# Order of mixer work and weight splits on ScalarE and VectorE in a hybrid decoder layer, with the joined moves of slots, banks and gate rows

## The chip, the cores and the metric

One core of one Trainium2 chip. The metric is the device time of one launch in microseconds, median of the runs shown. Activations, weights and states are fp32.

## The reference, cut to what matters

One inference step of one layer: RMSNorm, one wide projection, two token mixers side by side (gated DeltaNet with 8 heads, mLSTM with 8 heads), a gated merge, an output projection, and a gated ConvFFN. There are 256 prompt tokens (fresh state) and 8 sample sequences of 4 tokens that continue a state.

```python
proj = h @ w_in
g_qkv, g_z, g_a, g_b, m_qkv, m_i, m_f, m_o, gate_a, gate_b = jnp.split(proj, idx, axis=-1)
c, new_gdn_conv = _causal_dwconv(g_qkv, gdn_conv_buf, gdn_conv_w)
c = jax.nn.silu(c)
...
go, new_gdn_S = _gated_delta_chunked(gq, gk, gv, g, beta, gdn_S.astype(f32))
go = _rmsnorm(go.transpose(0, 2, 1, 3), gdn_norm_w) * jax.nn.silu(g_z...)
y_a = go.reshape(B, T, GDN_V).astype(x.dtype) @ w_branch_a
...
mh, new_C, new_n, new_m = _mlstm_chunked(mq, mk, mv, ig, lf, ...)
y_b = mh.astype(x.dtype) @ w_branch_b
mixed = jax.nn.sigmoid(gate_a) * y_a + jax.nn.sigmoid(gate_b) * y_b
x = x + mixed @ w_out
```

## The kernel before, in words

All 288 tokens (256 prompt, 32 sample) lie along the free axis, so activations are stored transposed, 128 channels to a tile. A weight matmul multiplies a 128x128 block of weights by a 128x288 block of activations, and is done as three matmuls of rounded parts (`product`, lines 1914 to 1916): high weight part by high activation part, high by low, low by high.

**Weights.** SP loads them in units of 16 blocks of 128x128 into `w_raw`. Four of these blocks are one ring block. For each, ScalarE (ACT) makes the high part, `split_hi` (line 633, `w_hi`), VectorE (DVE) makes the low part, `split_lo` (line 640, `w_lo`), and PE multiplies. The ring has four places: in slot s, ACT and DVE make the block of slot s+3, once PE is through with slot s-1 (semaphore `blocks`). So three blocks lie ready ahead of PE at most.

**The front stage** is the projection by `w_in` with both mixers woven in: 384 slots of 12 matmuls each, four slots to a tile of 128 columns, 16 to a quad of four tiles. `ORDER` gives the quads: DeltaNet heads (q, k, v, z), mLSTM heads, and at the end gates. A finished tile is taken out of PSUM and scaled by DVE (`evacuate`, line 1484) in the first slot behind it; a consumer waits by `in_place(kind, i, m)` until tile m of a quad (0 to 3) is out.

Each engine has its own hand-written program for the front, and `front(eng, each, lanes, lanes_first)` (line 483) weaves it: in each slot it runs `each(slot)` (the engine's weight work) and lets every lane go on up to this slot. A lane is a generator, and `yield n` means that what follows is due n slots behind the lane's start. Lanes are `gates_rows` (from slot 0), `prepare(h)` for DeltaNet head h (from slot 17+28h), `scan(h)` (from 45+28h) and `mlstm(i)` (from 274+14i). Below, "phase n" is n slots behind a lane's start. On PE the lanes of a slot come ahead of its products, on ACT and DVE the weight split comes ahead of the lanes, and POOL has only lanes. A scan of head h runs in the same 28 slots as the preparation of head h+1: phase n of one is phase n of the other.

Names that the change and the steps touch:

- `prepare`: POOL copies the last columns of q, k, v (lines 774, 775), from which PE takes the convolution's state rows (line 1895); DVE and ACT form the convolution (lines 1521, 988), ACT applies Silu to it and to z (lines 1003 to 1008, with a table load ahead and one behind, 1000 and 1009); the squares' low part `sq_lo` (line 1524) feeds the norms on PE (line 1977); then come six levels of a triangular inverse, in which DVE forms `x_xt`, `decay` and `nt` (lines 1595, 1587) and PE multiplies pairs (lines 2012, 2018, 2021).
- `scan`: PE forms the output's sums (`nrm`, line 2075, from `sqo_lo`, line 1632); ACT makes the reciprocal root in two steps `rs1` and `rs2`; DVE scales by it (`go`, three instructions, line 1637); POOL multiplies by z (`goz`, line 820); ACT and DVE make the high and low parts of the result (line 1648 the low one). PE forms the state's update for 8 sequences (`Ss`, line 2085), and DVE adds it in, eight instructions `S_sample` (line 1644); ACT starts the stores of the states.
- `gates_rows`: DVE's row work on the mLSTM gates (lines 1414 to 1447), ACT's exponentials, and PE's turning of rows to columns (`cols`, `cols2`).

**Behind the front** comes the branch stage (`w_branch_a`, `w_branch_b`): each of its products' accumulators is a PSUM bank, `ps[:, 2 * (u % 2) + k % 2]`, which DVE's `first` and `second` multiply by the gates (lines 1736, 1742). The out stage (`w_out`) follows, and then the ConvFFN, which the change does not touch.

Of the kernel before, what the change touches and what calls it, by code (L numbers as in the profile page):

```python
# [7 lines left out]
P = 128  # L8
# [57 lines left out]
def build(nc, a, o):  # L66
# [3 lines left out]
    KT = D // P  # L70
# [56 lines left out]
    with ctx:  # L127
# [238 lines left out]
        scan_d = Steps(sem("scan_dve"), "S0 R1 S1 rs sql go ss1 ss2 lo")  # L366
# [116 lines left out]
        def front(eng, each, lanes, lanes_first=False):  # L483
            for slot in range(SLOTS):
                if lanes_first:
                    for lane in lanes:
                        lane.upto(slot)
                each(slot)
                if not lanes_first:
                    for lane in lanes:  # L490
                        lane.upto(slot)
            for lane in lanes:
                lane.finish()
# [196 lines left out]
        def _(pool):  # L690
# [77 lines left out]
            def prepare(h):  # L768
                x4, kq, xx, ec, g = *handed[h % 2][:2], *handed[h % 2][-2:], gq[h % 2]
                yield 0  # L770
                pool.wait_ge(*in_place("g", h))
                if h:
                    pool.wait_ge(*prep_t.after("last", h - 1))
                pool.tensor_copy(g_last[:, 0:3 * GPAD].rearrange("p (t s) -> p t s", t=3), g[:, :, TP:TP + GPAD]).then_inc(*prep_p.done("la"))
                pool.tensor_copy(g_last[:, 3 * GPAD:].rearrange("p (t b s) -> p t b s", t=3, s=GPAD),
                                 seqs3(g[:, :, GPAD + TP:], GS, L, GS)).then_inc(*prep_p.done("lb"))
                yield 5
                pool.wait_ge(*prep_a.after("si2", h))
                pool.tensor_tensor(sq[:], qkv[:, 0:2], qkv[:, 0:2], ALU.mult).then_inc(*prep_p.done("sq"))
# [24 lines left out]
                pool.tensor_copy(in_four(x4[0:TS]), fourfold(xx[0:TS, 1, TP:T])).then_inc(*prep_p.done("x4"))  # L804

            def scan(h):
                yield 12
                pool.wait_ge(*scan_a.after("vn_s", h))
                if h:
                    pool.wait_ge(*scan_t.before(h))  # L810
                else:
                    for steps in (gate_d, gate_a, gate_t):
                        pool.wait_ge(*steps.before(1))
                    pool.wait_ge(stored, 32)
                pool.tensor_tensor(vnm[:], vn_s[:].unsqueeze(1).to_broadcast([P, 2, P]),
                                   seq2[:].unsqueeze(2).to_broadcast([P, 2, P]), ALU.mult).then_inc(*scan_p.done("vnm"))
                yield 19
                pool.wait_ge(*scan_d.after("go", h))
                apart(pool)
                pool.tensor_tensor(gout[:], gout[:], zt[h % 3][:], ALU.mult).then_inc(*scan_p.done("goz"))  # L820
# [82 lines left out]
        def _(act):  # L903
# [13 lines left out]
            def gates_rows():  # L917
# [46 lines left out]
                yield 35  # L964
# [6 lines left out]
                yield 37  # L971
# [7 lines left out]
            def prepare(h):  # L979
# [3 lines left out]
                act.wait_ge(*in_place("g", h))  # L983
# [23 lines left out]
                yield 4  # L1007
                nc.scalar.activation(zt[h % 3][:], zt[h % 3][:], ACT.Silu).then_inc(*prep_a.done("sz"))
# [42 lines left out]
            def scan(h):  # L1051
# [21 lines left out]
                yield 17  # L1073
                act.wait_ge(*scan_a.after("rs1", h))
                nc.scalar.activation(rso[:], rso[:], ACT.Exp, scale=-0.5).then_inc(*scan_a.done("rs2"))
                yield 20
# [7 lines left out]
                yield 22  # L1084
                act.wait_ge(*scan_d.after("ss2", h))
# [83 lines left out]
            act.wait_ge(cs_out, 32 * H)  # L1169

# [18 lines left out]

            for n in range(3, 7):  # L1190
                split_hi(q_out, n, 8)
# [132 lines left out]
        def _(dve):  # L1324
# [33 lines left out]
            def gates_rows():  # L1358
# [55 lines left out]
                yield 21  # L1414
# [5 lines left out]
                yield 23  # L1420

                g("mm1", scan_rows(mmx[:], anew[:, 2], c_row[:], 0.0, ALU.add, ALU.max))
                g("mm2", tt(seqd(mmx[:]), at_seq(m_in), seqd(mmx[:]), ALU.max))
                g("bl1", tc(f_row[:, 0:1], b_row[:, TP - 1:TP]))
                g("bl2", tc(one_col(f_row[:, 1:]), seqd(b_row[:])[..., L - 1:]))
# [3 lines left out]
                yield 35  # L1429
# [4 lines left out]
                yield 36  # L1434
                g("sw1", ts(sw_row[:, 0:TP], c_row[:, 0:TP], mxl[:, 0:1], None, ALU.subtract))
                g("sw2", tt(seqd(sw_row[:]), seqd(c_row[:]), at_seq(mxl), ALU.subtract))
                yield 38
# [3 lines left out]
                yield 41  # L1441
# [53 lines left out]
            def prepare(h):  # L1495
# [8 lines left out]
                if h == 0:  # L1504
                    yield 0

                    for n, t in enumerate((handed[1][0][:], handed[1][4][:, TP:T], r_s[:])):
                        nc.vector.memset(t, 0.0).then_inc(pads_zero, 1)
                    dve.wait_ge(pads_zero, 3)
# [36 lines left out]
                yield 12  # L1546
                halves = [(P, slice(0, TP)), (TS, slice(TP, T))]
# [63 lines left out]
            def scan(h):  # L1611
# [21 lines left out]
                yield 18  # L1633
# [5 lines left out]
                for k in range(2):  # L1639
                    yield 20 + k  # L1640
                    dve.wait_ge(*scan_t.after("Ss", h))

                    for b in range(4 * k, 4 * k + 4):
                        last = stt(ss[:, b], ss[:, b], ec[:, NCH + b:NCH + b + 1], S_BANKS[b // 2][:, b % 2 * P:(b % 2 + 1) * P], ALU.mult, ALU.add)  # L1644
                    d(f"ss{k + 1}", last)
                yield 21
                dve.wait_ge(*scan_a.after("hi", h))
                d("lo", tt(one(go_lo, h), gout[:], one(go_hi, h).bitcast(F32), ALU.subtract))

# [81 lines left out]
            with dve.Fori(0, 4) as i:  # L1731
                def first(h, c):
                    m = 2 * h + c
                    dve.wait_ge(blocks, 16 * (i + q_branch) + (8 * h + 4))
                    dve.wait_ge(*br_a.after(f"sa{m}", i))
                    tt(mix_a[:, m], one(gates, 4 * i + m), ps[:, c, 0:T], ALU.mult).then_inc(bank_free, 1)

                def second(h, c):
                    m = 2 * h + c
                    dve.wait_ge(blocks, 16 * (i + q_branch) + (8 * h + 8))  # L1740
                    dve.wait_ge(*br_a.after(f"sb{m}", i))
                    tt(mix_b[:, m], one(gates, 4 * i + m + KT), ps[:, 2 + c, 0:T], ALU.mult).then_inc(bank_free, 1)
                    dve.wait_ge(*freed(2 * i + (g_branch + h), 2 + c))
                    tt(mix_b[:, m], mix_b[:, m], mix_a[:, m], ALU.add).then_inc(*br_d.done(f"s{m}"))
# [145 lines left out]
        def _(pe):  # L1890
# [27 lines left out]
            def gates_rows():  # L1918
# [43 lines left out]
                yield 39  # L1962
# [3 lines left out]
            def prepare(h):  # L1966
# [58 lines left out]
                if h:  # L2025
                    pe.wait_ge(*scan_d.after("ss2", h - 1))
# [121 lines left out]
            def weights(slot):  # L2148
# [6 lines left out]
                for k in range(4):  # L2155
# [6 lines left out]
                  lanes_first=True)  # L2162
# [26 lines left out]
            pe.wait_ge(bank_free, 4 * g_branch + 4)  # L2189


            with pe.Fori(0, 4) as i:
                for u in range(4):
                    x_hi, x_lo = ((go_hi, go_lo), (mh_hi, mh_lo))[u % 2]
                    pe.wait_ge(bank_free, 8 * i + (4 * g_branch + 2 * u + 2))
                    if u == 1:
                        pe.wait_ge(*md_.before(H))
                    for j in range(4):
                        pe.wait_ge(lo_ready, 16 * (i + q_branch) + (4 * u + j + 1))
                        for k in range(4):  # L2200
                            kk = 2 * j + k // 2
                            last = product(ps[:, 2 * (u % 2) + k % 2, 0:T], whi[:, j, k], wlo[:, j, k], x_hi[:, kk], x_lo[:, kk],
                                           kk == 0, kk == 7)
                        last.then_inc(blocks, 1)
# [14 lines left out]
            with pe.Fori(0, 4) as i:  # L2219
                turn_input(i)  # L2220

                pe_group(i + q_out, i + g_out, mix_hi, mix_lo, ring=8, x_last=br_d.before(4))
# [153 lines left out]
```

## Time and profile before

| | us |
|---|---|
| median of 3 runs | 1874.73 (1874.36 to 1876.82) |
| the profiled execution's own time | 1879.15 |
| its span in the trace | 1877.1 |
| PE busy in the span | 1852.0 (99%) |
| VectorE (DVE) busy | 1226.8 (65%) |
| ScalarE (ACT) busy | 921.4 (49%) |
| GpSimd (POOL) busy | 156.7 (8%) |
| mean granted TensorE clock | 0.996 |

The profile is of one execution. The front ends at 801.4 us of the span, the branch stage at 905.9 us. Busy shares are averages over the span; "PE" counts matmuls, "PEld" their weight loads, which overlap. On a row of the timeline the number in brackets is how long the engine had been idle, and what released it.

### The profile page before, as it was taken

What the parts mean: (1) busy time and instruction counts of PE and PEld (TensorE: products, weight loads), DVE (VectorE), ACT (ScalarE), POOL (GpSimd) and SP (SyncE); (2) the same over time, 40 slices, a digit from 0 to 9 for tenths busy, and PEclk for the clock granted to TensorE, in tenths of its full rate; (3) what the DMA queues carried; (4) which work ended last, traced back from release to release, by engine and by line L of the source; (5) the groups of instructions that cost most, each with busy time, mean ns of one, the idle gap of its engine ahead of it and who ended that gap; (6) DMA issues with size and microseconds to landing.
All of it is one profiled execution on the core that took longest, in us unless ns stands there. A gap on an engine that the chain in (4) does not pass through costs nothing.

```text
span 1877.1 us, 38358 instructions
## 1 busy us (share of the span) xinstructions
PE 1852.0 (99%) x14078; PEld 1820.5 (97%) x14078; DVE 1226.8 (65%) x2714; ACT 921.4 (49%) x1837; POOL 156.7 (8%) x324
## 2 busy tenths in 40 slices
PE   9999999999999999999999999999999999999998
PEld 7899999999999999999999999999999999999998
DVE  5877777777756667666655766754666764566753
ACT  5554455554544554555545444543454443454553
POOL 4001010100100101100121000000000000000022
PEclk8999999999999999999999999999999999999999
DMA  8456556555567667556675656576555666556562
GB/s 228 133 148 163 145 161 162 160 158 158 148 157 196 172 180 191 149 172 187 177 203 151 166 153 164 157 193 171 160 159 157 180 164 174 162 155 161 141 179 75
DMA packets 572817, 308.25 MB, mean 164 GB/s; under 512 B 10607, under 2 KB 567815, under 8 KB 572695
## 3 DMA queue, kind: packets, MB, share of 16 engines
q1 hardware_dynamic: 531571, 281.24, 55.5%
q10 hardware_dynamic: 41124, 25.39, 4.9%
q8 instruction: 76, 1.25, 0.3%
q14 instruction: 46, 0.38, 0.1%
HBM read 293.58 MB, written 13.02 MB: 163 GB/s over the span
## 4 chain that ended last, share of the span: by engine, by line
PE 93%; DVE 4%; ACT 1%; issue 1%; DMA 0%; SPq 0%; ACTq 0%; POOL 0%; DVEq 0%
PE products L1914 29%; PE products L1916 28%; PE products L1915 28%; PE mixer L1895 2%; DVE w_lo L640 1%; ACT w_hi L633 1%; DVE S_sample L1644 1%; PE mixer L2012 1%; PE products L2353 0%; DVE gdn_out L1637 0%; DMA x_s_rows<-in_x_sample 0%; PE products L2085 0%; PE mixer L2018 0%; DVE x_xt L1595 0%; PE products L2056 0%
## 5 line engine op out<-in xcount | busy, mean ns | idle before, releaser
L640 DVE TENSOR_TENSOR w_lo<-w_raw,w_hi 128x512 fp32r<-128x512 f32 x1037 | 716.1, 706 | 554.6 <-ACT w_hi L633 550.2
L633 ACT ACTIVATE w_hi<-w_raw 128x512 fp32r<-128x512 f32 x1037 | 629.5, 626 | 565.4 <-PE products L1916 545.2
L1914 PE MATMUL products<-h_hi,w_hi 128*128 128x288 f32 x1536 | 476.8, 310 | 0.1
L1915 PE MATMUL products<-h_lo,w_hi 128*128 128x288 f32 x1536 | 455.7, 297 | 0.0
L1916 PE MATMUL products<-h_hi,w_lo 128*128 128x288 f32 x1536 | 454.5, 296 | 0.0
L1914 PE MATMUL products<-f_hi,w_hi 128*128 128x288 f32 x1408 | 417.4, 296 | 0.0
L1915 PE MATMUL products<-f_lo,w_hi 128*128 128x288 f32 x1408 | 416.1, 295 | 0.0
L1916 PE MATMUL products<-f_hi,w_lo 128*128 128x288 f32 x1408 | 415.2, 295 | 0.0
L1914 PEld LDWEIGHTS products<-h_hi,w_hi 128*128 128x128 f32 x1536 | 290.9, 189 | 9.0 <-issue 7.2
L1915 PEld LDWEIGHTS products<-h_lo,w_hi 128*128 128x128 f32 x1536 | 291.3, 190 | 0.0
L1916 PEld LDWEIGHTS products<-h_hi,w_lo 128*128 128x128 f32 x1536 | 291.0, 189 | 0.0
L1916 PEld LDWEIGHTS products<-f_hi,w_lo 128*128 128x128 f32 x1408 | 265.3, 188 | 0.0
L1915 PEld LDWEIGHTS products<-f_lo,w_hi 128*128 128x128 f32 x1408 | 264.5, 188 | 0.1
L1914 PEld LDWEIGHTS products<-f_hi,w_hi 128*128 128x128 f32 x1408 | 264.2, 188 | 0.1
L1914 PE MATMUL products<-u_hi,w_hi 128*128 128x288 f32 x704 | 210.4, 299 | 0.0
L1915 PE MATMUL products<-u_lo,w_hi 128*128 128x288 f32 x704 | 208.1, 296 | 0.0
L1916 PE MATMUL products<-u_hi,w_lo 128*128 128x288 f32 x704 | 207.6, 295 | 0.0
L1916 PEld LDWEIGHTS products<-u_hi,w_lo 128*128 128x128 f32 x704 | 132.7, 188 | 0.0
L1915 PEld LDWEIGHTS products<-u_lo,w_hi 128*128 128x128 f32 x704 | 132.3, 188 | 0.0
L1914 PEld LDWEIGHTS products<-u_hi,w_hi 128*128 128x128 f32 x704 | 132.1, 188 | 0.0
L1914 PE MATMUL products<-mix_hi,w_hi 128*128 128x288 f32 x256 | 76.1, 297 | 0.0
L1915 PE MATMUL products<-mix_lo,w_hi 128*128 128x288 f32 x256 | 75.7, 296 | 0.0
(486 smaller groups left out, 2183.2 us busy)
## 6 DMA issues: line engine op xcount, KB each, us to landing
w_raw<-in_w_in SPq DMA_DIRECT2D x95, 1024.0 KB, 6.0
w_raw<-in_w_up SPq DMA_DIRECT2D x88, 1024.0 KB, 5.9
w_raw<-in_w_down SPq DMA_DIRECT2D x32, 1024.0 KB, 5.9
w_raw<-in_w_out SPq DMA_DIRECT2D x16, 1024.0 KB, 6.5
w_raw<-in_w_down SPq DMA_DIRECT2D x16, 768.0 KB, 4.9
w_raw<-in_w_branch_a SPq DMA_DIRECT2D x8, 1024.0 KB, 5.4
w_raw<-in_w_branch_b SPq DMA_DIRECT2D x8, 1024.0 KB, 5.4
S_sample<-in_state_gdn_S ACTq DMA_DIRECT2D x8, 512.0 KB, 5.8
```

What stands on the lines that cost most here:

```text
L633: nc.scalar.activation(ring_slot(whi, whi2, n, ring), raw[:, s % slots, 4 * j:4 * j + 4], ACT.Copy).then_inc(hi_ready, 1)
L640: nc.vector.tensor_tensor(ring_slot(wlo, wlo2, n, ring), raw[:, s % slots, 4 * j:4 * j + 4], ring_slot(whi, whi2, n, ring).bitcast(F32), A ...
L1644: last = stt(ss[:, b], ss[:, b], ec[:, NCH + b:NCH + b + 1], S_BANKS[b // 2][:, b % 2 * P:(b % 2 + 1) * P], ALU.mult, ALU.add)
L1895: return nc.tensor.transpose(out, in_, ident[0:n, 0:n])
L1914: mm(out, w_hi, x_hi, start=start, stop=False)
L1915: mm(out, w_hi, x_lo, start=False, stop=False)
L1916: return mm(out, w_lo, x_hi, start=False, stop=stop)
L2012: mm(pm[:, 2, 0:P], nt[:, 0:P], cols_of(xx[:, 0], 1 << l), start=True, stop=True).then_inc(*prep_t.done(f"p{l}"))
```

## The change

`front` gets the slot from which lanes come first: slot 45 (`SCAN_AT[0]`) for ACT and DVE, 0 for PE, and POOL has no weight work. Up to slot 44 ACT and DVE do the split first as before. Joined to it:

1. `Steps` of the scan on DVE get a third group of the state's update, `ss3`. The update of 8 sequences was 4 in phase 20 and 4 in phase 21, with the low part of the result behind it in 21; now it is 2 in phase 20, 3 in 21, the low part in 22, 3 in 23. ACT's two stores of the states go from phase 22 to 24; PE's last level of the next head waits for `ss3` in place of `ss2`.
2. `rs2` on ACT moves from phase 17 into 16, `go` on DVE from 18 to 17, `goz` on POOL from 19 to 18, the high part on ACT from 20 to 19.
3. POOL's and ACT's first step of `prepare` waits for tiles q, k, v alone (`in_place("g", h, 2)`); ACT waits for z ahead of its Silu in phase 4.
4. For head 0 three memsets of padding move from DVE to POOL, and DVE waits for them in phase 12.
5. `gates_rows`: DVE's rows move from phases 21, 23, 35, 36, 38 and 41 to 32, 34 with 36, 38, 40, 42 and 45; ACT's from 35 and 37 to 39 and 41; PE's `cols2` from 39 to 43.
6. Branch stage: PE waits for the last readers of its banks in the mixers and not for the last gate tile's evacuation; the two pairs of banks are exchanged; at the start of the out stage PE waits for the branch's last evacuation. ACT waits for its stores of the mLSTM states ahead of the out stage's splits and not ahead of the branch stage.

```diff
-        def front(eng, each, lanes, lanes_first=False):
+        def front(eng, each, lanes, lanes_first=SCAN_AT[0]):
             for slot in range(SLOTS):
-                if lanes_first:
+                if slot >= lanes_first:
                     for lane in lanes:
                         lane.upto(slot)
                 each(slot)
-                if not lanes_first:
+                if slot < lanes_first:
...
-                pool.wait_ge(*in_place("g", h))
+                pool.wait_ge(*in_place("g", h, 2))
...
+                if h == 0:
+                    yield 1
+                    pool.wait_ge(*st_t.after("small3"))
+                    for t in (handed[1][0][:], handed[1][4][:, TP:T], r_s[:]):
+                        pool.memset(t, 0.0).then_inc(pads_zero, 1)
...
-                yield 19
+                yield 18
                 pool.wait_ge(*scan_d.after("go", h))
...
-                act.wait_ge(*in_place("g", h))
+                act.wait_ge(*in_place("g", h, 2))
...
                 yield 4
+                act.wait_ge(*in_place("g", h))
                 nc.scalar.activation(zt[h % 3][:], zt[h % 3][:], ACT.Silu).then_inc(*prep_a.done("sz"))
...
-                yield 17
                 act.wait_ge(*scan_a.after("rs1", h))
...
-                yield 20
+                yield 19
                 act.wait_ge(*scan_p.after("goz", h))
...
-                yield 22
-                act.wait_ge(*scan_d.after("ss2", h))
+                yield 24
+                act.wait_ge(*scan_d.after("ss3", h))
...
-            act.wait_ge(cs_out, 32 * H)
-
             nc.scalar.preload_act_table(ACT.Sigmoid)
...
-                yield 18
+                yield 17
                 dve.wait_ge(*scan_a.after("rs2", h))
...
-                for k in range(2):
-                    yield 20 + k
-                    dve.wait_ge(*scan_t.after("Ss", h))
-
-                    for b in range(4 * k, 4 * k + 4):
-                        last = stt(ss[:, b], ss[:, b], ec[:, NCH + b:NCH + b + 1], S_BANKS[b // 2][:, b % 2 * P:(b % 2 + 1) * P], ALU.mult, ALU.add)
-                    d(f"ss{k + 1}", last)
+
+                def samples(name, first, last):
+                    for b in range(first, last):
+                        done = stt(ss[:, b], ss[:, b], ec[:, NCH + b:NCH + b + 1], S_BANKS[b // 2][:, b % 2 * P:(b % 2 + 1) * P], ALU.mult, ALU.add)
+                    d(name, done)
+                yield 20
+                dve.wait_ge(*scan_t.after("Ss", h))
+                samples("ss1", 0, 2)
                 yield 21
+                samples("ss2", 2, 5)
+                yield 22
                 dve.wait_ge(*scan_a.after("hi", h))
                 d("lo", tt(one(go_lo, h), gout[:], one(go_hi, h).bitcast(F32), ALU.subtract))
+                yield 23
+                samples("ss3", 5, NB)
...
-                    tt(mix_a[:, m], one(gates, 4 * i + m), ps[:, c, 0:T], ALU.mult).then_inc(bank_free, 1)
+                    tt(mix_a[:, m], one(gates, 4 * i + m), ps[:, 2 + c, 0:T], ALU.mult).then_inc(bank_free, 1)
...
-            pe.wait_ge(bank_free, 4 * g_branch + 4)
-
+            pe.wait_ge(*md_.after("cs4", H - 1))
+            pe.wait_ge(*ma.after("cp", H - 1))
...
-                            last = product(ps[:, 2 * (u % 2) + k % 2, 0:T], whi[:, j, k], wlo[:, j, k], x_hi[:, kk], x_lo[:, kk],
+                            last = product(ps[:, 2 * ((u + 1) % 2) + k % 2, 0:T], whi[:, j, k], wlo[:, j, k], x_hi[:, kk], x_lo[:, kk],
...
                 turn_input(i)
 
+                pe.wait_ge(bank_free, 4 * g_out + 4)
                 pe_group(i + q_out, i + g_out, mix_hi, mix_lo, ring=8, x_last=br_d.before(4))
```

## Rows read from the trace of the kernel before

**Rows 1.** What PE waited for, whole span: us in total, times, longest.

```profile
PE products L2085 <- DVE gdn_out L1637: 4.9, 8, 0.7
PE mixer L2012 <- DVE x_xt L1595: 4.3, 8, 1.1
PE mixer L1895 <- POOL gdn_last_cols L775: 2.1, 1, 2.1
...
PE products L1914 <- DVE gates L1484: 1.4, 1, 1.4
...
PE products L2075 <- DVE sqo_lo L1632: 0.6, 1, 0.6
```

**Rows 2.** Windows: us, busy (count) of PE, PEld, DVE, ACT, POOL, PEclk, DMA, GB/s.

```profile
62.70:66.50 3.80, 3.80 (x18) 3.80 (x19) 3.71 (x10) 2.66 (x7) 0.00 (x0) 0.55 1.01 274
289.65:346.59 56.94, 55.88 (x439) 54.03 (x437) 42.87 (x114) 29.62 (x62) 6.03 (x14) 1.00 0.59 159
```

**Rows 3.** PE's timeline in one head's 28 slots: start, us, line.

```profile
323.87 0.29 PE L1916 MATMUL products<-h_hi,w_lo 128*128 128x288 f32 x1
...
324.13 0.38 PE L1914 MATMUL products<-h_hi,w_hi 128*128 128x288 f32 x1
...
327.51 0.29 PE L1916 MATMUL products<-h_hi,w_lo 128*128 128x288 f32 x1
...
329.41 0.40 PE L1914 MATMUL products<-h_hi,w_hi 128*128 128x288 f32 x1
...
332.79 0.30 PE L1916 MATMUL products<-h_hi,w_lo 128*128 128x288 f32 x1
...
333.21 0.38 PE L1914 MATMUL products<-h_hi,w_hi 128*128 128x288 f32 x1
...
336.57 0.29 PE L1916 MATMUL products<-h_hi,w_lo 128*128 128x288 f32 x1
...
337.57 0.38 PE L1914 MATMUL products<-h_hi,w_hi 128*128 128x288 f32 x1
...
651.61 0.29 PE L1916 MATMUL products<-h_hi,w_lo 128*128 128x288 f32 x1
...
652.48 0.40 PE L1914 MATMUL products<-h_hi,w_hi 128*128 128x288 f32 x1
```

**Rows 4.** The chain of waits, 325 to 336 us: start, length, what.

```profile
327.90 0.74 DVE gdn_out L1637 x3
...
335.07 1.03 DVE S_sample L1644 x4
```

**Rows 5.** PE's timeline at the start, the branch stage and the out stage.

```profile
78.70 0.40 PE L1977 MATMUL mixer<-sq_hi,ones 128*128 128x288 f32 x1 [0.70 <-DVE sq_lo L1524]
...
803.01 0.40 PE L1914 MATMUL products<-go_hi,w_hi 128*128 128x288 f32 x1 [1.36 <-DVE gates L1484]
...
905.99 0.38 PE L1914 MATMUL products<-mix_hi,w_hi 128*128 128x288 f32 x1
```

**Rows 6.** DVE's timeline at the start, in one head, and at the out stage.

```profile
75.97 0.74 DVE L1422 TENSOR_TENSOR_SCAN m_max<-anew,c_row 8x288 f32<-8x288 f32 x1
...
77.89 0.76 DVE L1524 TENSOR_TENSOR sq_lo<-sq,sq_hi 128x576 fp32r<-128x576 f32 x1
...
325.53 0.28 DVE L1587 TENSOR_TENSOR decay<-beta_decay,mask_level 128x128 f32<-128x128 f32 x1
...
329.53 0.53 DVE L1587 TENSOR_TENSOR nt<-beta_decay,mask_level 128x128 f32<-128x128 f32 x1
...
906.35 0.45 DVE L1742 TENSOR_TENSOR mix_b<-gates,products 128x288 f32<-128x288 f32 x1
```

**Rows 7.** Groups of instructions in 289.65 to 346.59: busy, mean ns, idle before.

```profile
L633 ACT ACTIVATE w_hi<-w_raw 128x512 fp32r<-128x512 f32 x28 | 17.6, 630 | 26.4 <-PE products L1916 26.3
L1521 DVE SCALAR_TENSOR_TENSOR conv_out<-gdn_qkv,gdn_conv_w_t,conv_out 128x312 f32<-128x312 f32 x9 | 4.3, 540 | 0.0
...
L1000 ACT ACT_TABLE_LOAD x1 | 1.3, 1283 | 0.0
```

More of the change, by code:

```diff
@@ L365, in build @@
         scan_a = Steps(sem("scan_act"), "vn0 vn1 ks_s vn_s sqo sqh rs1 rs2 hi")
-        scan_d = Steps(sem("scan_dve"), "S0 R1 S1 rs sql go ss1 ss2 lo")
+        scan_d = Steps(sem("scan_dve"), "S0 R1 S1 rs sql go ss1 ss2 lo ss3")
         scan_p = Steps(sem("scan_pool"), "vnm goz")
@@ L963, in gates_rows @@
                 act.dma_start(grow[:].rearrange("p r t -> p (r t)"), to_all(g_scr, 0, 3 * T)).then_inc(grow_in, 16)
-                yield 35
+                yield 39
                 act.wait_ge(*gate_d.after("wi1"))
@@ L970, in gates_rows @@
                 nc.scalar.activation(m_row[:, 2 * T + TS:], m_row[:, 2 * T + TS:], ACT.Exp).then_inc(*gate_a.done("fw"))
-                yield 37
+                yield 41
                 act.wait_ge(*gate_d.after("sw2"))
@@ L1187, in _ @@
                 group(split_hi, i + q_branch, [(-1, lambda: sigs(0)), (9, lambda: upper(0)), (9, lambda: sigs(1)), (15, lambda: upper(1))])
+            act.wait_ge(cs_out, 32 * H)
             for n in range(3, 7):
@@ L1413, in gates_rows @@
                 g("nbB", ts(nbeta[0:TS, 2], cols[0:TS, 1, 2], -1.0, None, ALU.mult))
-                yield 21
+                yield 32
                 at_seq = lambda t: t[:, 1:].unsqueeze(2).to_broadcast([H, NB, L])
@@ L1419, in gates_rows @@
                 g("c", tt(c_row[:], ig[:], b_row[:], ALU.subtract))
-                yield 23
+                yield 34
                 g("mm1", scan_rows(mmx[:], anew[:, 2], c_row[:], 0.0, ALU.add, ALU.max))
@@ L1424, in gates_rows @@
                 g("bl1", tc(f_row[:, 0:1], b_row[:, TP - 1:TP]))
+                yield 36
                 g("bl2", tc(one_col(f_row[:, 1:]), seqd(b_row[:])[..., L - 1:]))
@@ L1428, in gates_rows @@
                 g("mnew", tt(m_new[:], f_row[:], mxl[:], ALU.add))
-                yield 35
+                yield 38
                 g("negmx", ts(m_row[:, 0:T], mmx[:], -1.0, None, ALU.mult))
@@ L1433, in gates_rows @@
                 g("fw", tt(m_row[:, 2 * T + TS:], m_in[:, 1:], mxl[:, 1:], ALU.subtract))
-                yield 36
+                yield 40
                 g("sw1", ts(sw_row[:, 0:TP], c_row[:, 0:TP], mxl[:, 0:1], None, ALU.subtract))
                 g("sw2", tt(seqd(sw_row[:]), seqd(c_row[:]), at_seq(mxl), ALU.subtract))
-                yield 38
+                yield 42
                 dve.wait_ge(*gate_a.after("sw"))
@@ L1440, in gates_rows @@
                 g("ksc", ts(sw_row[:], sw_row[:], QSCALE, None, ALU.mult))
-                yield 41
+                yield 45
                 dve.wait_ge(*gate_t.after("cols2"))
@@ L1502, in d @@
                         step(prep_d, name, h)
[L1504 to L1509, printed above, removed]
                 for j in range(1, GC):
@@ L1546, in prepare @@
                 yield 12
+                if h == 0:
+                    dve.wait_ge(pads_zero, 3)
                 halves = [(P, slice(0, TP)), (TS, slice(TP, T))]
@@ L1741, in second @@
                     dve.wait_ge(*br_a.after(f"sb{m}", i))
-                    tt(mix_b[:, m], one(gates, 4 * i + m + KT), ps[:, 2 + c, 0:T], ALU.mult).then_inc(bank_free, 1)
+                    tt(mix_b[:, m], one(gates, 4 * i + m + KT), ps[:, c, 0:T], ALU.mult).then_inc(bank_free, 1)
                     dve.wait_ge(*freed(2 * i + (g_branch + h), 2 + c))
@@ L1961, in gates_rows @@
                 columns(pm[:, 2], GPARTS, (g_row[:, 0], g_row[:, 2], e_row[:]), e4[:]).then_inc(*gate_t.done("cols"))
-                yield 39
+                yield 43
                 pe.wait_ge(*gate_d.after("ksc"))
@@ L2025, in prepare @@
                 if h:
-                    pe.wait_ge(*scan_d.after("ss2", h - 1))
+                    pe.wait_ge(*scan_d.after("ss3", h - 1))
                 mm(pm[:, 1, 0:P], psb[:, 0:P], rows_of(xx[:, 1], 64), start=True, stop=True)\
@@ L2161, in _ @@
                   + [Lane(SCAN_AT[h], scan(h)) for h in range(H)] + [Lane(MLSTM_AT[i], mlstm(i)) for i in range(H)],
-                  lanes_first=True)
+                  lanes_first=0)
             def column_tile(q, b0, n, bank, free, x_hi, x_lo, ring, mixer=None, stages=0, b_all=0, n_all=16, x_last=None):
```

## The prediction

> **What bounds the kernel now.** I read the page's busy shares first: PE is busy 99% of the span, so a gain must come from the places where PE stands, and those are few. The list of PE's waits [rows 1] names them: two kinds with DVE as releaser that recur in the DeltaNet heads (`Ss` behind `go`, 4.9 us in 8 waits; a pair behind `x_xt`, 4.3 us in 8), and single ones of 2.1 us (POOL's columns), 1.4 us (last gate tile) and 0.6 us (`nrm`). PE's busy time flatters it: a matmul that is late is drawn long. So I took gaps from PE's timeline, from the start of a slot's last product to the start of the next slot's first [rows 3]. Unstalled products follow each other by 0.13 us, which the window over one head gives as 439 matmuls in 55.88 us [rows 2].
>
> **The repeated gaps, heads 0 to 6** [rows 3]. In phase 19 PE goes from 327.51 to 329.41, 1.90 us, over a pair and `Ss`. What these need unstalled: a pair alone takes 0.26 (323.87 to 324.13), and an update of the same form (8 matmuls of 32x256, in an mLSTM head) 0.87 (651.61 to 652.48), together 1.00 when the common step of 0.13 is taken off once. So 0.90 is stall. Phase 23: 1.00 (336.57 to 337.57) less 0.26 is 0.74. Phase 21: 0.42 (332.79 to 333.21) less 0.26 is 0.16, and phase 25 is like it. The sum is 1.96 us a head. The gaps repeat to 0.01 us in seven heads.
>
> What holds them is shown by the chain of waits [rows 4]: DVE's three `go` (0.74) end just ahead of `Ss`, and they, like the pair's `x_xt`, stood behind the split of that slot; in phase 23 four `S_sample` (1.03), the low part and a split stood ahead of `x_xt`. The change takes the split from ahead of both: the mixer work now runs as soon as PE has released it, and the split behind it has three ready blocks as cover, 3 x 12 x 0.13 = 4.7 us. `go` also comes a phase (about 1.8 us) earlier, more than the stall of 0.90; and `S_sample` is spread 2, 3, 3, so that phase 21 carries 3 x 0.26 rather than 4, and phase 23 its last three behind the pair's work of the same slot. I take all of it: 7 x 1.96 = **13.7**. The ends: one pair's stall stays (0.16 and 0.25, some 0.4 a head, 3 us less), nothing more than 13.7 above, since that is all the stall there is.
>
> **Head 7's scan** has no inverse beside it. Its stalls are 0.6 (`nrm` behind `sqo_lo`) [rows 1], with restart 0.9, and `Ss` about 0.7, the longest of its row. Taken as **1.6** (0.7 to 1.6).
>
> **The start, slots 17 to 44.** POOL's column copies wait for all four tiles of the quad, PE waits for them 2.1 us [rows 1], and behind that wait the granted clock falls to 0.55, the lower level (1.2 GHz), for 3.8 us [rows 2], in which 18 matmuls run that need 18 x 0.13 = 2.3; so 1.5 more. With z left out of the wait, POOL starts when v is out, some slots earlier, and both go: 3.5 at most. But PE then meets the next limit, `sq_lo`, for which it already waits 0.70 [rows 5]: DVE does gate rows from 75.97 until 77.89, when `sq_lo` starts [rows 6]. Those rows move to phases 32 and later, which frees 1.9. So here 1.9 to 3.5; I take 3.0, near the upper end, because three more gate rows of phase 21 leave the same stretch. The rows land in slots 32 to 45, where the first pair waits 1.1 today (the longest of its row [rows 1]): that shrinks, and new short waits of 0.3 to 0.4 appear where the moved rows stand ahead of `x_xt`; net +0.4, between -0.7 and +1.1. Together **3.4** (1.2 to 4.6). The memsets go to POOL, idle then, and their wait comes at phase 12, 20 us behind: nothing. PE's `cols2` and ACT's exponentials move with them, long before the mLSTM heads read them: nothing; without that cover, mlstm_first would wait.
>
> **Branch stage.** PE's wait for the last gate tile, 1.36, is replaced by two that ended long before, in banks the gate tiles do not use first: **+1.4** (1.0 to 1.4, since DVE's evacuation now competes with the first splits). ACT's wait for the mLSTM stores moves behind this stage; ACT has three ready blocks as cover, and if that were gone the wait is hidden still by the stage's 100 us. At the out stage the bank exchange puts PE behind the branch's last `second`: the first product started at 905.99 and that evacuation runs 906.35 to 906.80 [rows 5, 6], so **-0.9** (0 to -0.9).
>
> **At nothing.** ACT's `rs2` in phase 16 is three instructions that only come earlier; the state stores leave two phases later (two more DMA starts on ACT's queue in phase 24 rather than 22), and nothing reads them until the next load of the same tile, five phases on. SP's queue is not touched: a split comes later inside its slot, so a unit's load may start up to a slot later, but a unit is four slots. mLSTM heads: their gaps of 5.5 us a head are PE's own work, and DVE or ACT releases none of it.
>
> **The lock.** `goz` on POOL now meets a split. Before, it ran beside `nt`, which took 0.53 where the like instruction took 0.28 [rows 6]: 0.25 lost. If 0.25 falls on the path it is 0.25 x 8 = 2.0; I put it at 0, because the pair behind it has 0.3 to spare. The Trainium skill ("SBUF — State Buffer", section "Who interferes with whom") says that a VectorE instruction with two SBUF inputs and a GpSimd one that reads SBUF exclude each other for a whole instruction. That agrees with the 0.53 beside 0.28; by it the split and `goz` would queue, whichever came first, and it is a rival below.
>
> **Sum**: 13.7 + 1.6 + 3.4 + 1.4 - 0.9 = 19.2. The profiled execution took 1879.15, so 1859.95 in its terms; it lies 4.42 above the median of the runs shown, so a median of 1855.5. About 0.2% (3.7 us) is what a measurement of this kernel can tell from no change.
>
> **Rivals.** (1) *The splits become late, slower.* In phases 2 to 7 ACT now does the convolution's part, two table loads (1.28 each) and Silu ahead of the splits, DVE nine convolution instructions (4.3) [rows 7]. Only the ready blocks cover that. Laying ACT's and DVE's instructions of one head out in the new order with their own durations, the closest block (slot 136) is ready about 1 us ahead of PE; so if the convolution ends more than 1 us later than in that layout, PE waits for `w_lo`, and each further us costs 1 us in each of 8 heads. To be slower than before it must eat 19.2 / 8 = 2.4 a head, a slip of 3.4; at 4 the loss is 3.0 x 8 = 24, and the time 1855.5 + 24 = 1879.5. For it: the two table loads stand in adjacent slots, and ACT's w_hi (0.63) must follow each. Against: ACT is busy 29.6 of 56.9 us in a head [rows 2] and waits 26.3 of it for PE [rows 7], and so catches up at once. Chance 0.04. (2) *Part of it*: the same lateness at 0.5 to 1 us a head beyond the spare 1 us, or `x_xt` still late because in phases 20 to 24 DVE has some 10 us of work by its own rows (five splits, eight `S_sample`, evacuations, the inverse) where PE needs some 9: 4 to 8 us kept back, 1859.5 to 1863.5. Chance 0.25. (3) *The lock on the path*: POOL and DVE queue in phase 18 of each head, 2.0 us (0.25 x 8): 1857.5, or 1859.5 at twice that. Chance 0.12. (4) *The change does nothing*, since DVE and not its order is the bound in the stalled phases: the gaps shift and stay, 1874.7. DVE is busy 42.9 of 56.9 [rows 2], which speaks against it. Chance 0.03. The forecast has 0.56.
>
> **How the numbers follow.** The likeliest case gives 1855.5. Below, the start at its best (4.6) and the out stage at no loss give 1.2 + 0.9 less, 1853.4; two more for unknowns in PE's own restart, 1851.5. Above, cases (2) and (3) reach to 1863.5, with the start at its low end (2.2 less) 1865.5. That leaves cases (1) and (4) and the tails out, under 0.2. Faster by over 0.2% (below 1871): 0.93; within: 0.03; slower: 0.04.
>
> **What would show it.** After: the rows `Ss` behind `go` and pair behind `x_xt` gone from the list of PE's waits or under 1 us each; phase 19 at about 1.0 and phases 21, 23, 25 at 0.26; the window with clock 0.55 gone; the branch's first product 0.2 behind the front's last; a new wait of 0.7 to 0.9 at the out stage. Wrong: waits of products (lines 1914 to 1916) for `w_lo` or `w_hi` in phases 5 to 8 of each head, or the head's 28 slots longer than 56.9 less 2.0 = 55.0 us.

## The result and the profile after

The changed kernel takes 1855.76 us (median of 4 runs, 1853.84 to 1859.10), the kernel before 1875.47 beside it: a ratio of 0.9896, 95% interval 0.9882 to 0.9910. The prediction was 1855.5. The profiled execution took 1859.10 with a span of 1857.2, 19.9 less than the 1877.1 of before. PE's line numbers are 5 higher in the changed kernel: the products are lines 1919 to 1921, the pairs 2017 and 2023, `Ss` 2090. DVE's `x_xt` (1595) and `go` (1637) keep theirs.

First the list of what PE waited for, over the whole span of the changed kernel (us in total, times, longest):

```profile
PE products L1919 <- DVE w_lo L640: 1.2, 1, 1.2
...
PE products L1919 <- DVE mix_b L1747: 0.8, 1, 0.8
...
PE products L2061 <- DMA S_sample<-in_state_gdn_S: 0.2, 1, 0.2
PE mixer L2017 <- DVE x_xt L1595: 0.2, 1, 0.2
```

Of the five waits in [rows 1], four are gone, and the second is down from 4.3 us in 8 waits to 0.2 in one. Three are new: one wait for a weight split, 1.2, one at the out stage, 0.8, in the place that the prediction named, and a short one for a load of `S_sample`, 0.2.

PE's timeline in the same head as [rows 3], from the last product of phase 18 to the first of phase 19, and then phases 22 and 23:

```profile
317.68 0.29 PE L1921 MATMUL products<-h_hi,w_lo 128*128 128x288 f32 x1
317.81 0.38 PE L2017 MATMUL mixer<-x_xt,decay 128*128 128x128 f32 x2
318.12 0.48 PE L2090 MATMUL products<-v_new_by_seq,kg 32*128 32x256 f32 x2
...
318.76 0.40 PE L1919 MATMUL products<-h_hi,w_hi 128*128 128x288 f32 x1
...
323.97 0.29 PE L1921 MATMUL products<-h_hi,w_lo 128*128 128x288 f32 x1
324.10 0.38 PE L2023 MATMUL mixer<-p_sb 128*128 128x128 f32 x2
324.24 0.38 PE L1919 MATMUL products<-h_hi,w_hi 128*128 128x288 f32 x1
```

Phase 19 is 1.08 us (317.68 to 318.76) where it was 1.90, and the pairs follow a product without a gap. DVE's timeline of the same stretch shows the new order: `go` and `x_xt` each ahead of the split of its slot.

```profile
315.11 0.76 DVE L1637 SCALAR_TENSOR_TENSOR gdn_out<-mixer,gdn_norm_w_t,rs_o 128x128 f32<-128x128 f32 x3
315.79 0.68 DVE L640 TENSOR_TENSOR w_lo<-w_raw,w_hi 128x512 fp32r<-128x512 f32 x1
316.41 0.29 DVE L1595 TENSOR_TENSOR x_xt<-x_xt,mixer 128x128 f32<-128x128 f32 x1
316.73 0.31 DVE L1602 STREAM_TRANSPOSE p_sb<-x_xt 128x128 f32<-128x128 f32 x1
316.96 0.74 DVE L640 TENSOR_TENSOR w_lo<-w_raw,w_hi 128x512 fp32r<-128x512 f32 x1
317.62 0.50 DVE L1587 TENSOR_TENSOR nt<-beta_decay,mask_level 128x128 f32<-128x128 f32 x1
```

POOL's `goz` of this head, to which e1 comes back:

```profile
316.02 1.13 POOL L825 TENSOR_TENSOR gdn_out<-gdn_out,z 128x288 f32<-128x288 f32 x1 [12.21 <-DVE gdn_out L1637]
```

Cutting the span at the starts of the same products in each trace gives a table that the rest leans on. "Heads 0 to 6" is slot 45 to slot 241, seven periods of 28 slots; the columns are us.

| kernel | to slot 17 | 17 to 45 | heads 0 to 6 | head 7 | mLSTM rest | to branch | branch to out |
|---|---|---|---|---|---|---|---|
| before | 58.70 | 60.11 | 399.08 | 50.82 | 232.65 | 1.65 | 102.97 |
| changed | 58.88 | 55.27 | 386.15 | 49.16 | 232.50 | 0.13 | 103.94 |
| split first (e1) | 55.15 | 55.28 | 396.26 | 50.07 | 232.61 | 0.13 | 103.94 |
| order alone (e2) | 54.60 | 60.46 | 385.84 | 49.16 | 232.50 | 1.67 | 103.58 |
| rows early (e3) | 54.57 | 59.57 | 385.84 | 49.16 | 232.50 | 0.13 | 103.94 |
| wait for z (e4) | 54.61 | 55.76 | 385.84 | 49.16 | 232.50 | 0.13 | 103.94 |
| go late (e5) | 57.71 | 55.27 | 386.44 | 49.16 | 232.50 | 0.13 | 103.94 |
| samples 4+4 (e6) | 55.88 | 55.28 | 385.84 | 49.16 | 232.50 | 0.13 | 103.94 |
| branch as before (e7) | 54.86 | 55.26 | 385.84 | 49.16 | 232.50 | 1.63 | 102.97 |
| lanes first from 17 (e8) | 54.45 | 54.66 | 385.84 | 49.16 | 232.50 | 0.13 | 103.94 |
| two more loads (e13) | 54.72 | 57.83 | 394.90 | 49.16 | 232.50 | 0.13 | 103.94 |
| three edits (e16) | 54.93 | 54.72 | 385.84 | 49.16 | 232.50 | 0.13 | 102.87 |

From the out stage's first product to the last weight product, 966.8 us on, all of them agree to 0.1 us; from there to the end of the span, with the last stores, they take 3.0 to 4.5. What else differs between executions of one kernel lies ahead of slot 17 (the last section comes to that), but for a wait in head 0 that stands at e5. The start gives 4.8, heads 0 to 6 12.9, head 7 1.7, the branch stage's start 1.5, and the out stage takes 1.0 back: 19.9.

### The profile page after: what moved, and what is told of

The parts are those of the page before. It is cut to its first block, busy times and chain, and to the rows that moved or that the text cites. A ratio compares the mean times of both kernels' runs of the same rounds, so it can differ in the third digit from the quotient of the medians.

```text
span 1857.2 us, 38358 instructions
## 1 busy us (share of the span) xinstructions
PE 1844.5 (99%) x14078; PEld 1817.6 (98%) x14078; DVE 1231.3 (66%) x2711; ACT 917.3 (49%) x1837; POOL 160.4 (9%) x327
## 3 DMA queue, kind: packets, MB, share of 16 engines
q8 instruction: 76, 1.25, 0.3%
## 4 chain that ended last, share of the span: by engine, by line
PE 97%; DVE 1%; DMA 1%; ACT 0%; issue 0%; SPq 0%; ACTq 0%; DVEq 0%
PE products L1919 30%; PE products L1921 29%; PE products L1920 29%; PE mixer L1900 2%; PE mixer L2017 1%; DMA S_sample<-in_state_gdn_S 1%; PE mixer L2023 1%; PE products L2359 0%; DMA x_s_rows<-in_x_sample 0%; DVE w_lo L640 0%; PE mixer L2150 0%; PE products L2090 0%; PE products L2061 0%; PE products L1900 0%; DVE conv_out L1519 0%
```

## The experiments

**e1: the splits ahead again, all else as changed.**

```diff
-        def front(eng, each, lanes, lanes_first=SCAN_AT[0]):
+        def front(eng, each, lanes, lanes_first=SLOTS):
```

> The changed kernel with the weight splits ahead of the lanes on ACT and DVE throughout, as before; slots, banks and gate rows stay as changed. Theory (order and joined moves each hold part): x_xt of a slot then ends about 1.7 us behind the last product of the slot before (w_hi 0.63, w_lo 0.69, x_xt 0.28 and the steps between), a little more than a slot of 1.58, so the pairs of phases 19, 21, 23 and 25 come 0.16 late each; go, a phase earlier, no longer holds Ss. A DeltaNet head then takes 55.12 + 4 x 0.16 = 55.8 us, the whole kernel 1855.8 + 8 x 0.64 = about 1861. Rival 1 (the order alone makes the gain in the heads): the head is back at 56.9 us, the kernel at about 1855.8 + 14 = 1870. Rival 2 (the joined moves alone make it): head 55.1, kernel 1856.

Measured: 1866.43 us (5 runs), ratio to before 0.9956 (0.9941 to 0.9970); a head takes 56.52. So about half of the gain is gone, and 56.94 to 56.52 is all that the joined moves give the heads without the order: nearer to the first rival than to the theory, which expected 55.8. Phases 21 and 23 came as expected, 0.42 each where the changed kernel has 0.27. Phases 19 and 25 did not. Phase 25 rose from 0.42 to 0.65: its `x_xt` now stands behind the three `S_sample` (0.86) of phase 23 and a split. So, without the order, the joined moves take 0.57 from phase 23 and give 0.23 back in phase 25. Phase 19 fell by only 0.1, from 1.90 to 1.80. DVE's timeline of this kernel shows why, and POOL's beside it:

```profile
317.55 1.26 DVE L640 TENSOR_TENSOR w_lo<-w_raw,w_hi 128x512 fp32r<-128x512 f32 x1 [0.24 <-ACT w_hi L633]
318.73 0.28 DVE L1595 TENSOR_TENSOR x_xt<-x_xt,mixer 128x128 f32<-128x128 f32 x1
```

```profile
317.45 0.81 POOL L825 TENSOR_TENSOR gdn_out<-gdn_out,z 128x288 f32<-128x288 f32 x1 [12.94 <-DVE gdn_out L1637]
```

```profile
319.06 0.49 PE L2017 MATMUL mixer<-x_xt,decay 128*128 128x128 f32 x2 [0.45 <-DVE x_xt L1595]
```

`goz` started 0.10 ahead of the split, and the split took 1.26 where it takes 0.69 alone; the pair behind it waited 0.45 and `Ss` behind the pair. It is so in all eight heads: split issued 0.09 to 0.10 behind `goz`, 1.25 to 1.28 long. This is the lock, on the path, in a kernel where it was not looked for; the earlier `goz` and the split ahead of the lanes meet there. The Trainium skill ("SBUF — State Buffer", section "Who interferes with whom") says that the shared ports are an exclusive lock and that the order of issue decides who is blocked. The split's 1.26 behind `goz` agrees, and so does the changed kernel: there the split at 315.79 is issued 0.23 ahead of `goz` (316.02) and takes 0.68, and `goz` takes 1.13 where it took 0.81.

**e2: the order alone, on the kernel before.**

```diff
-        def front(eng, each, lanes, lanes_first=False):
+        def front(eng, each, lanes, lanes_first=SCAN_AT[0]):
...
-                if lanes_first:
+                if slot >= lanes_first:
...
-                if not lanes_first:
+                if slot < lanes_first:
...
-                  lanes_first=True)
+                  lanes_first=0)
```

> The kernel before with one thing changed: from slot 45 on ACT and DVE do the lanes ahead of the split. Theory: go in phase 18 now ends ahead of Ss, the pairs' x_xt come ahead of the splits, but four S_sample and the low part in phase 21 still push later work on: head about 55.3 us (1.6 gained of 1.82), start and branch stage unchanged, kernel about 1875.5 - 8 x 1.6 = 1862.7. Rival (the joined moves make the gain, or four S_sample in one slot make the splits late): head 56.5 us or more, kernel above 1871.

Measured: 1860.13 (4 runs), ratio 0.9920 (0.9903 to 0.9936). The head takes 55.12, just what it takes in the changed kernel, better than the 55.3 expected. In the heads the order is the whole gain. The kernel pays elsewhere: branch to out takes 103.58 in place of 102.97. ACT's timeline at the branch stage's start, and the chain of waits there:

```profile
786.65 1.28 ACT L1171 ACT_TABLE_LOAD   x1 [4.19 <-DMA out_s_C<-C_sample]
787.94 0.63 ACT L633 ACTIVATE w_hi<-w_raw 128x512 fp32r<-128x512 f32 x1
```

```profile
781.34 5.22 DMA out_s_C<-C_sample
...
787.94 0.64 ACT w_hi L633
788.58 0.02 issue
788.61 0.70 DVE w_lo L640
789.31 0.04 issue
789.35 0.40 PE products L1914
```

ACT stood 4.19 us for the store of the last mLSTM state, and the three ready blocks were used up before the next one came: PE lost 0.35 there and 0.27 at the block behind it (791.21), the 0.61 in all. In e7, which has the same PE side but the wait moved, the stretch takes 102.97. So moving that wait behind the branch stage, which the prediction put at nothing, is worth the difference once the order is changed.

**e5 and e6: the scan's joined moves undone one by one.** e5 puts `rs2`, `go`, `goz` and the high part back by a phase; e6 puts the state's update back to 4 and 4.

```diff
...
-                yield 17
+                yield 18
                 dve.wait_ge(*scan_a.after("rs2", h))
```

> The changed kernel with the scaling chain a phase later, as before: rs2 in phase 17, go in 18, goz on POOL in 19, the high part in 20; the lanes still ahead of the splits. Theory: go then ends at the start of slot 18, a slot ahead of Ss, so phase 19 stays at 1.1 us and the head within 0.1 us of 55.12. Rival (the earlier phase is what frees Ss): phase 19 at 1.5 us or more, head 55.6 or more, kernel 4 us slower.

```diff
-                samples("ss1", 0, 2)
-                yield 21
-                samples("ss2", 2, 5)
...
+                for k in range(2):
+                    yield 20 + k
+                    dve.wait_ge(*scan_t.after("Ss", h))
+                    for b in range(4 * k, 4 * k + 4):
```

> The changed kernel with the state's update as 4 in phase 20 and 4 in phase 21 and the low part behind it in 21, as before; all else as changed. Theory: phases 20 to 24 hold as much DVE work in all, only bunched in 21 (1.1 us of S_sample, 0.45 low part, x_xt, split), so PE waits 0.2 to 0.5 us in phase 22 or 23; head 55.3 to 55.6, kernel 2 to 4 us slower. Rival (the spread is idle decoration, the three ready blocks cover it): head 55.12, no difference.

Measured, one execution each: 1857.42 and 1854.95; the head is 55.12 in both, phase for phase as in the changed kernel. (In e5 head 0 took 0.6 longer, a wait of 0.5 for the first load of `S_sample`; the changed kernel's first profile has one of 0.2, the others none.) So the theory held for e5; for e6 it did not, and the rival did: bunched work in phase 21 is covered. No product waits there for the split that it delays, which has three ready blocks ahead of it.

**e3 and e4: the start.** e3 puts the gate rows back to their phases (DVE 21 for 32, and so on), e4 lets POOL and ACT wait for z again.

```diff
-                yield 32
+                yield 21
                 at_seq = lambda t: t[:, 1:].unsqueeze(2).to_broadcast([H, NB, L])
...
```

> The changed kernel with the gate rows at their old phases (DVE 21, 23, 35, 36, 38, 41; ACT 35, 37; PE 39). Theory (the start gains 4.7 us up to slot 45 because both the columns come early and sq_lo no longer stands behind the rows): sq_lo is then held again, PE waits for it 1 to 2 us more at slot 26, and the scan of head 0 begins 1.5 to 2.5 us later than with the change (its slot 45 at about 116.2 in place of 114.15). Rival (the early columns alone make the gain): slot 45 within 0.5 us of 114.15.

```diff
-                pool.wait_ge(*in_place("g", h, 2))
+                pool.wait_ge(*in_place("g", h))
...
-                act.wait_ge(*in_place("g", h, 2))
+                act.wait_ge(*in_place("g", h))
```

> The changed kernel with POOL's and ACT's first step of prepare waiting for z again. Theory: the wait of 2.1 us for POOL's columns at slot 18 and the lower clock behind it (18 matmuls in 3.8 us) come back, slot 21 begins 3.5 us later; of this the wait for w_lo at slot 24 (1.2) falls away, so slot 45 is 2.3 to 3.5 us later. Rival (sq_lo would bind there anyway, and the early columns only bring the wait forward): slot 45 less than 1 us later.

These have to be read from slot 17, not by slot 45's place as the expectations put it, since what comes ahead of slot 17 differs by 4 us between executions. From slot 17 to slot 45 e3 takes 59.57, 4.30 more than the changed kernel, where the theory had 1.5 to 2.5: with the columns early, the rows are nearly the whole of the start's gain. Of the 4.30, slots 17 to 29 have 2.9 and slots 29 to 45 1.4. The list of waits and PE's timeline of e3 name what they held:

```profile
PE mixer L2016 <- DVE x_xt L1594: 1.3, 1, 1.3
PE mixer L1981 <- DVE sq_lo L1521: 1.3, 1, 1.3
```

```profile
73.78 0.40 PE L1981 MATMUL mixer<-sq_hi,ones 128*128 128x288 f32 x1 [1.33 <-DVE sq_lo L1521]
```

PE gets there earlier than before and waits longer. e4 takes 55.76, only 0.49 more: the wait of 2.1 for the columns is back, and yet most of the time is not, which is the rival's result. What bound there instead is not `sq_lo`, as the rival had it, but the 1.2 for `w_lo` that the changed kernel has and e4 has not.

The clock has a part in this. In e4's one execution it stayed at 1.00 behind the wait (the last section has the windows); in the kernel before and in e2 it fell, and slots 18 and 19 took 5.45 and 5.33 us where e4's took 3.94. No run has the moved rows, the wait and the lower clock together. With these 1.4 to 1.5 on top of 0.49 the columns would be worth about 2.0, an estimate from these rows.

What led to that 1.2 shows in DVE's and POOL's timelines of the changed kernel, ahead of PE's wait:

```profile
70.53 1.04 DVE L1416 TENSOR_SCALAR minus_beta<-token_cols 128x16 f32<-128x16 f32 x1
71.61 0.22 DVE L1417 TENSOR_SCALAR minus_beta<-token_cols 32x8 f32<-32x8 f32 x1
71.86 0.69 DVE L640 TENSOR_TENSOR w_lo<-w_raw,w_hi 128x512 fp32r<-128x512 f32 x1
```

```profile
70.39 1.15 POOL L784 TENSOR_TENSOR sq<-qkv 128x576 f32<-128x576 f32 x1 [17.39 <-ACT qkv L1010]
```

```profile
72.69 0.37 PE L1919 MATMUL products<-h_hi,w_hi 128*128 128x288 f32 x1 [1.22 <-DVE w_lo L640]
```

An instruction over 16 columns took 1.04 and ended with POOL's square; in e2, with POOL idle, the same instruction took 0.17. With 0.17 here the split, whose `w_hi` was ready at 70.83, would have started 0.87 earlier, an estimate of its share in the 1.22. Against this wait, at the full clock, the early columns are worth 0.5.

**e7: the branch stage as before.**

```diff
...
-            pe.wait_ge(*md_.after("cs4", H - 1))
-            pe.wait_ge(*ma.after("cp", H - 1))
+            pe.wait_ge(bank_free, 4 * g_branch + 4)
...
-                pe.wait_ge(bank_free, 4 * g_out + 4)
```

> The changed kernel with the branch stage's PE side as before: PE waits for the last gate tile, the banks not exchanged, no wait at the out stage. Theory: the branch begins 1.5 us later after the front's last product (1.65 in place of 0.14) and the out stage's first product comes 0.9 to 1.0 earlier after it (about 103.0 in place of 103.9): 0.5 to 0.6 us slower in all. Rival: the wait at the out stage is not of the exchange (the turning of x is late as well), then 1.5 slower.

Measured: 1.63 to the branch stage and 102.97 from there to the out stage, one execution at 1855.14. The theory held to 0.1: the exchange of banks gives 1.50 and takes 0.97, 0.5 in all.

**e8: lanes first from slot 17.** `lanes_first=PREP_AT[0]`, nothing else.

> The changed kernel with the lanes ahead of the splits already from slot 17, where head 0's prepare begins. Theory: pairs at slots 34, 40 and 43, which are 0.5, 0.2 and 0.7 late because x_xt and the moved gate rows stand behind a split, come earlier (about 1 us gained), the wait for w_lo at slot 24 (1.2) stays or grows by up to 1, since convolution, Silu and two table loads now stand ahead of the splits: slot 45 between 1 us earlier and 0.5 later. Rival (late splits): waits for w_lo at slots 22 to 26 of 2 us or more in all, slot 45 later than 115.

Measured: slots 17 to 45 in 54.66, 0.61 less than changed: 1.3 less in slots 29 to 45 and 0.7 more in slots 17 to 29. The late pairs at slots 34 and 40 went, as expected; the 1.2 wait was replaced by two of 0.7 at slots 20 and 23. Slot 43's 0.7 stayed: it is PE's own turning of the rows, which moved there with `cols2`.

**e13: the price of the slower rival.** Two table loads more in phase 3 of each head; they compute nothing.

```diff
+                nc.scalar.preload_act_table(ACT.Sigmoid)
+                nc.scalar.preload_act_table_set(EXP_LN)
                 nc.scalar.preload_act_table(ACT.Silu)
```

> The changed kernel with two table loads more on ACT (to Sigmoid and back to the exponentials) ahead of the load for Silu in phase 3 of each head, 2 x 1.28 = 2.57 us of ACT time that computes nothing. It prices the slower rival. Theory as predicted (the closest split has about 1 us to spare): each of heads 1 to 7 loses about 1.5 us at slots 7 to 9 of the preparation, as waits of products for w_lo; the kernel about 12 us slower than with the change. Rival (the cover is wider than the layout by hand made it, since the loads run while ACT would wait for PE): under 0.3 us a head, no more than 2 us in all.

Measured: 1866.32, one execution; 394.90 in heads 0 to 6, that is 9.06 more. ACT's timeline in one head and PE's, of this kernel:

```profile
287.74 1.28 ACT L1005 ACT_TABLE_LOAD   x1
289.03 1.28 ACT L1006 ACT_TABLE_LOAD   x1
290.32 1.28 ACT L1007 ACT_TABLE_LOAD   x1
```

```profile
294.56 0.40 PE L1921 MATMUL products<-h_hi,w_hi 128*128 128x288 f32 x1 [0.81 <-DVE w_lo L640]
```

In that head 2.57 more on ACT cost 1.08 (56.20 against 55.12), so 1.5 was to spare; so it is in four of the seven periods. In two it cost 1.38, and in the first 1.97, where only 0.6 was to spare. In slots 17 to 45, where the splits come first and `w_lo` is waited for already, all of the 2.57 shows (57.83 against 55.26). That is 11.6 in all, near the 12 of the theory, but a fifth of it lies in a stretch that the theory had not named. The rival's mechanism is real, and the spare is 0.6 to 1.5 where the prediction had 1.

**e14 to e16: three further edits.** Lanes first from slot 17; Silu's table load at the end of phase 2; and the out stage's four banks turned by two, so that its first tile uses bank 2, free since the branch's first half, and the new wait goes.

```diff
-                pe.wait_ge(bank_free, 4 * g_out + 4)
-                pe_group(i + q_out, i + g_out, mix_hi, mix_lo, ring=8, x_last=br_d.before(4))
+                pe_group(i + q_out, i + g_out, mix_hi, mix_lo, ring=8, x_last=br_d.before(4), turned=2)
...
+            pe.wait_ge(bank_free, 4 * g_ffn + 3)
...
-                yield 3
                 nc.scalar.preload_act_table(ACT.Silu)
+                yield 3
```

> The changed kernel with three further edits, each in its own stretch: lanes first on ACT and DVE from slot 17; the table load for Silu issued at the end of phase 2, where ACT waits for PE, and not in phase 3; the out stage's four banks turned by two (first tile in bank 2, which the branch's first half leaves free), so that PE waits for nothing at its start. Theory: slots 17 to 45 take 53.4 to 54.3 us (54.66 with the lanes alone, 55.27 with the change; the w_lo waits of 0.7 at slots 20 and 23 shrink); heads stay at 55.12; branch to out 102.97 in place of 103.94, and no new wait at the ConvFFN's start: 1.9 to 2.8 us faster than with the change. Rival: the load at phase 2 displaces a split and the wait moves to slot 21 (54.7 or more), and the last out tile's bank is waited for at the ConvFFN's start (105.7 becomes 106.5).

One execution at 1853.78: branch to out 102.87, 1.07 less, and nothing given back at the ConvFFN (105.71); but slots 17 to 45 in 54.70, the 54.66 of e8. The table load was not what held slot 20: the wait there stays, and a third one for `w_lo` appears at slot 22, much as the rival had it. Then the changed kernel and the three edits were timed on one chip:

> The changed kernel itself, timed beside the kernel before on the chip of the next run. Theory: median 1855 to 1857, ratio 0.989 to 0.991; its segments as in its first profile (slots 17 to 45 55.27, heads 385.8 to 386.2, branch to out 103.94), and what differs between its executions lies ahead of slot 17 (54 to 59 us, with the granted clock there).

> The changed kernel with the three further edits (lanes first from slot 17, Silu's table in phase 2, the out stage's banks turned by two), as in the run before. Theory from its segments: 0.6 less in slots 17 to 45 and 1.1 less from branch to out, so 1.6 us under the changed kernel's median on the same chip (0.09%), near what the runs can tell. Rival: the segments' gain is given back in a part that a profile of one execution shows by chance, and the two medians agree within 0.5 us or the edits are slower.

The change again: 1854.58 (4 runs, 1854.03 to 1857.17), ratio 0.9894 (0.9877 to 0.9910). The three edits: 1852.95 (4 runs, 1851.42 to 1854.07), ratio 0.9881 (0.9864 to 0.9897). The medians differ by 1.63, as the segments say (0.52 and 1.07); the intervals overlap, so it is the segments that show this gain, not the ratio.

## Why the prediction was right, point by point

The sum was 19.2 and the profile shows 19.9. It came out so near partly because two errors stood against each other.

- **Heads 0 to 6**: 13.7 forecast, 12.9 measured. The four gaps closed by 0.82, 0.72, 0.15 and 0.15, and a period got 1.82 shorter, not 1.96: a pair with `Ss` takes 1.08, not the 1.00 that the mLSTM update stood for. The gaps do not repeat in all seven heads, as the prediction has it: in head 4 phase 25 is 0.72 and not 0.42, and heads 4 and 6 of before had 0.5 more to lose. The wait for `S_sample` in head 0 took 0.3 back.
- **The reason given for them** was too broad. The prediction listed three: the order, `go` a phase earlier, `S_sample` spread. e2, e5 and e6 show that the order alone does it, to 0.01 us a head, and that the other two add nothing to it. Without the order all the joined moves together give 0.4 a head (e1).
- **Head 7**: 1.6 forecast, 1.66 measured; in e1 its `nrm` wait stays and its `Ss` stall goes, in e2 both go. So the order takes the first, and either the order or the earlier `go` the second.
- **The start**: 3.4 forecast, 4.8 measured, above its upper end of 4.6; this is the term that was mis-sized. Slots 17 to 29 gave 3.7 where 3.0 was taken and 3.5 was the most, and slots 29 to 45 1.1 where a net of 0.4 was. And the cause was put first on the columns and the clock (3.5 at most), with the rows as the next limit. e3 and e4 turn that round. Each undone alone, the rows are worth 4.3 and the columns 0.5 at the full clock, or about 2.0, by the estimate at e4, where the clock falls; with the rows left early the columns, the clock and the memsets together give 0.5 (60.11 before, 59.57 in e3). So these prices do not simply add.
- **Branch and out stage**: +1.4 and -0.9 forecast, +1.52 and -0.97 measured, confirmed by e7.
- **At nothing**: held for the state stores and `cols2` at large (0.7 at slot 43 is what PE had done at slot 39); no run undoes the memsets alone. The ACT wait for the mLSTM stores was called hidden; e2 shows 0.6 for it where it was left in place, so it is not free.
- **The lock**: not on the path here (`w_lo` 0.74, `nt` 0.50, the pair on time), as forecast, but not for the spare time that the forecast gave as its reason: the split is issued ahead of `goz`, and `goz` is what gets longer. e1 shows that the order of issue decides it. In head 7 of the kernel before, `goz` had met a split already (1.26 long), and not `nt`.
- **The slower rival**: no such wait in the steady heads; e13 shows it begins when ACT is 0.6 to 1.5 later. One wait of that kind did come, 1.2 at slot 24, in the stretch where the splits still come first.
- **The range**: its upper end by its own terms is 1863.5 + 2.2 = 1865.7, not 1865.5; nothing hangs on it.

## What to carry to other kernels

Where a producer of ready-made input has a ring ahead of its consumer, and the same engine also answers that consumer in short round trips, do the round trips first: each one is on the path, and the ring work is not until its cover is used up. Price the cover by the longest run of other work that can now stand ahead of it, on each engine that feeds the ring; an otherwise idle store wait on one of them is such work too. And after a wait is removed, look in the same stretch for the next limit before counting it: here one wait of 2.1 us was worth 0.5 at the full clock.

## What the runs showed of the hardware that was not expected

**A short VectorE instruction held for a whole GpSimd one.** `minus_beta`, 128x16 with one input in SBUF, took 1.00 to 1.04 in the nine executions in which POOL's square (1.15) had started 0.13 to 0.18 ahead of it, and 0.17 to 0.18 in the four in which the square came later. In e4 the two started together; there it took 0.17, and the next one, 32x8, took 0.99. The prediction had looked for this only at `goz`.

**The clock behind a wait is not fixed by the wait.** In [rows 2] the granted clock falls to 0.55 behind PE's 2.1 us wait, and in e2 it does the same; in e4, with the same wait of 2.14, it does not. The windows of the 3.8 us behind the wait, e2's ahead of e4's:

```profile
58.40:62.20 3.80, 3.71 (x17) 3.71 (x18) 3.51 (x10) 2.30 (x6) 0.04 (x1) 0.56 0.91 256
```

```profile
58.40:62.20 3.80, 3.69 (x30) 3.53 (x30) 3.52 (x8) 2.90 (x7) 0.40 (x4) 1.00 0.94 257
```

What decides between them stays open.

**Most of the spread of the runs is the clock in the first 30 us.** The window from 13 to 20 us of the changed kernel's first profile, and of e15, the same kernel:

```profile
13.00:20.00 7.00, 7.00 (x27) 5.29 (x27) 3.52 (x6) 2.74 (x7) 5.45 (x24) 0.50 1.08 272
```

```profile
13.00:20.00 7.00, 7.00 (x46) 5.59 (x45) 4.97 (x10) 4.46 (x10) 5.70 (x19) 1.00 0.97 258
```

At 1.2 GHz PE does 27 matmuls there, at 2.4 GHz 46, and slot 17 begins at 58.88 or at 54.86. That is 4.0 us, most of the range of one kernel's runs (1853.84 to 1859.10), and the reason to compare edits of a microsecond by segments. The other traces agree: in the nine executions without a stretch at the lower clock there, slot 17 begins at 54.45 to 55.15, and in the five with one at 55.88 to 58.88.
